# Two-layer Mamba and attention trunk: the first modulation pieces divided 5 to 3, the norm's spread ahead of the columns, and unit 0 between the time-step products

## The chip, the core and the metric

The kernel runs on one core of a Trainium2 chip. The metric is the device time of one execution in microseconds (us); the median of the runs is compared. The engines are TensorE (PE, with its weight loads as PEld), VectorE (DVE), ScalarE (ACT), GpSimd (POOL) and SyncE (SP), which issues every DMA.

## What is computed

Two layers of a decoder trunk on 512 tokens of width 1024, all in float32:

```
ada = silu(c) @ w_ada[l] + b_ada[l]             # six vectors of 1024: sh1, sc1, g1, sh2, sc2, g2
h = rms_norm(x, norm1_g[l]) * (1 + sc1) + sh1
z, xbc, dt_raw, q, k, v, gate_s, gate_a = split(h @ w_in[l])
y_ssm = mamba2(z, silu(conv(xbc)), softplus(dt_raw + dt_bias), ...) @ w_ssm_out[l]
y_att = diff_attention(q, k, v, ...) @ w_attn_out[l]
x = x + g1 * ((sigmoid(gate_s) * y_ssm + sigmoid(gate_a) * y_att) @ w_out[l])
x = x + g2 * (relu(norm_and_modulate(x, sc2, sh2) @ w_ff1[l]) ** 2 @ w_ff2[l])
```

The end is one more rms_norm. What matters here is the start of a layer: the modulation `sh1`, `sc1`, the norm of x, the raw time steps `dt_raw` (32 columns of the input projection), their softplus and running sums, and the first units of the projection, which feed the convolution.

## The kernel before

The model dimension lies on the partitions in 8 blocks (KB) of 128, the 512 tokens along the free dimension. Each weight matrix is cut into **units** of 256 output columns. A unit is loaded in two halves into `raw` (SP), copied by ScalarE to `w_hi` (L901), and POOL subtracts the two for `w_lo` (L1746), so that float32 products are made of three: hi by hi, hi by lo, lo by hi (L553 to L555). `unit_rows` issues the six products of one block k of a unit, three for each of its two banks; eight such **parts** make a unit. Unit n uses slot n % 2 of the weights and banks gemm 0, 1 or 2, 3; it may not start before unit n - 2 has left its banks (`bank_free`). For the units of the convolution it is VectorE's third tap (L1410, `taps`) that frees them.

Order is written out by hand on each engine, with semaphores between them. The middle of a layer goes by ticks from T_FIRST = -10; `fill_of(tick)` says how many parts TensorE issues in a tick, four each in the first ones, so ticks -10 and -9 hold unit 0, and -8 and -7 unit 1.

**Modulation pieces.** The vector `ada` is computed in pieces of 256 columns; the first eight (FIRST, layer 0) give `sh1` and `sc1` and are needed before the first norm. Each piece is 1 MB of weights. A TensorE piece is 16 small products with one column (`ada_piece`, L605; the trace counts each twice). A VectorE piece is eight multiply-adds into `ada_acc[:, n % 2]` (L1286, L1290), and TensorE then sums its partitions in two products (`ada_column`, L613). The accumulator has two halves, and the VectorE piece n begins with

```
dve.wait_ge(ada_out, n - 1 + OUT_CREDIT)      # OUT_CREDIT = 2; each ada_column adds 1
```

that is, when column n - 2 is done. When the last column is in, `ada_full` releases VectorE's `take_ada` (L1297) and ScalarE's first conversion of a weight unit, since the TensorE pieces lay in the place of `w_hi` and `w_lo`.

**Norm of layer 0.** ScalarE squares x, VectorE adds the squares (L1267, L1269), TensorE sums over partitions (`norm_sum`, L626), VectorE scales (`norm_mean`, L1276), POOL takes the power (L1734), TensorE spreads the result over partitions (`norm_spread`, L634). Then `norm` goes over the eight blocks: VectorE makes `pre` (L1316), ScalarE `h_hi` (L928), VectorE `h_lo` (L1321).

**Time steps.** As `h_lo` of block k arrives, TensorE makes its three products with `dtw` (L664 to L666). After the last, ScalarE adds the bias (L965) and takes an exponential, and VectorE's chain makes the softplus and running sums from it (L1366 to L1399). Only behind that chain does VectorE's program have the taps of unit 0 (L1410). TensorE meanwhile goes on with units 0 and 1.

## Time and profile before

| | |
|---|---|
| median of 3 runs | 2591.09 us (2589.17 to 2594.97) |
| profiled execution | 2592.25 us, span 2590.5 us |
| TensorE busy | 2391.4 us, 92% |
| VectorE busy | 1417.7 us, 55% |
| ScalarE busy | 1007.8 us, 39% |
| POOL busy | 1090.6 us, 42% |
| mean rate of the transfers | 97 GB/s |

The span is the profiled execution from its first to its last instruction. A row of the timeline has start, duration, engine, line and operation, the tiles written and read, and in brackets how long the engine had been idle and who ended it. Runs of equal instructions are merged into one row (xN). Busy time of one engine is no bound by itself; what counts is which wait ends last at each place.

### The profile page before, as it was taken

The numbers are of one execution on the slowest core, as the hardware profiler recorded it, in microseconds if no ns is written. First come the engines' busy times: TensorE is split into PE (matmuls) and PEld (weight loads), VectorE is DVE, ScalarE is ACT, GpSimd is POOL, SyncE is SP. The second block draws the span as 40 slices with busy tenths as digits, with TensorE's granted clock in tenths as the row PEclk, the third lists the DMA queues.
The fourth block names the chain that finished last, engine by engine and source line by source line (L and its number), as shares of the span: only waits on it lengthen the run. The fifth ranks groups of instructions, "written<-read, shape, count | busy, mean of one in ns | idle before, by whom it ended". The sixth has DMA issues, their size and how long they took to land.

```text
span 2590.5 us, 32150 instructions
## 1 busy us (share of the span) xinstructions
PE 2391.4 (92%) x11866; PEld 1960.3 (76%) x11866; DVE 1417.7 (55%) x2047; ACT 1007.8 (39%) x1864; POOL 1090.6 (42%) x825
## 2 busy tenths in 40 slices
PE   7899998997789989999988999999878899899998
PEld 6677897876666868888866778988666678688886
DVE  6766666445554447778767676622555534422323
ACT  3355553344444233322334555533444443322322
POOL 1355543432223445454434645454322244444442
PEclk9899999998989989999999999999988999899999
DMA  6211124511111434455422121232111123222221
GB/s 231 77 58 51 65 81 130 195 66 49 58 41 66 147 114 166 179 195 191 167 97 67 52 71 50 80 100 90 49 57 49 57 86 118 74 97 98 94 94 57
DMA packets 84812, 250.27 MB, mean 97 GB/s; under 512 B 7472, under 2 KB 34480, under 8 KB 79280
## 3 DMA queue, kind: packets, MB, share of 16 engines
q1 hardware_dynamic: 84656, 248.22, 28.3%
q8 instruction: 94, 1.54, 0.2%
q14 instruction: 62, 0.51, 0.1%
HBM read 244.00 MB, written 4.19 MB: 96 GB/s over the span
## 4 chain that ended last, share of the span: by engine, by line
PE 42%; issue 21%; POOL 9%; DVE 9%; POOLq 8%; ACT 5%; DVEq 3%; DMA 1%; ACTq 1%; SPq 0%
POOL w_lo L1746 9%; POOLq L1748 8%; PE gemm L553 8%; PE gemm L555 8%; PE gemm L554 8%; PE aux L714 3%; PE gemm L576 2%; PE gemm L577 2%; PE gemm L578 2%; PE aux L618 2%; ACT swap L1059 2%; ACT probs L1116 1%; PE aux L701 1%; DVE smalls L1604 1%; PE aux L725 1%
## 5 line engine op out<-in xcount | busy, mean ns | idle before, releaser
L1746 POOL TENSOR_TENSOR w_lo<-raw,w_hi 128x512 fp32r<-128x512 f32 x704 | 965.1, 1392 | 1357.7 <-ACT w_hi L901 1350.5
L901 ACT ACTIVATE w_hi<-raw 128x1024 fp32r<-128x1024 f32 x352 | 371.0, 1057 | 759.3 <-PE gemm L555 692.2
L553 PE MATMUL gemm<-h_hi,w_hi 128*128 128x512 f32 x1504 | 619.2, 412 | 25.1 <-DVE conv L1410 19.7
L555 PE MATMUL gemm<-h_hi,w_lo 128*128 128x512 f32 x1504 | 598.3, 398 | 0.0
L554 PE MATMUL gemm<-h_lo,w_hi 128*128 128x512 f32 x1504 | 598.1, 398 | 0.0
L553 PEld LDWEIGHTS gemm<-h_hi,w_hi 128*128 128x128 f32 x1504 | 290.8, 193 | 108.5 <-issue 51.0
L555 PEld LDWEIGHTS gemm<-h_hi,w_lo 128*128 128x128 f32 x1504 | 289.7, 193 | 64.4
L554 PEld LDWEIGHTS gemm<-h_lo,w_hi 128*128 128x128 f32 x1504 | 290.7, 193 | 58.4 <-issue 1.9
L553 PE MATMUL gemm<-op_hi,w_hi 128*128 128x512 f32 x608 | 238.5, 392 | 0.2
L555 PE MATMUL gemm<-op_hi,w_lo 128*128 128x512 f32 x608 | 236.8, 389 | 0.0
L554 PE MATMUL gemm<-op_lo,w_hi 128*128 128x512 f32 x608 | 236.6, 389 | 0.0
L576 PE MATMUL gemm<-w_hi,h_hi 128*128 128x256 f32 x768 | 230.1, 300 | 3.8 <-ACT zh L1033 2.2
L577 PE MATMUL gemm<-w_hi,h_lo 128*128 128x256 f32 x768 | 220.8, 287 | 0.0
L578 PE MATMUL gemm<-w_lo,h_hi 128*128 128x256 f32 x768 | 220.6, 287 | 0.0
L1290 DVE SCALAR_TENSOR_TENSOR late_acc<-ada_late,first,late_acc 128x256 f32<-128x256 f32 x210 | 157.0, 748 | 7.5
L576 PEld LDWEIGHTS gemm<-w_hi,h_hi 128*128 128x128 f32 x768 | 151.6, 197 | 12.1 <-issue 12.0
L1116 ACT ACTIVATE probs<-aux,smalls 128x128 f32<-128x128 f32 (+3 forms) x128 | 66.4, 524 | 239.4 <-DVEq L1594 238.6
L577 PEld LDWEIGHTS gemm<-w_hi,h_lo 128*128 128x128 f32 x768 | 151.4, 197 | 2.5 <-issue 2.4
L578 PEld LDWEIGHTS gemm<-w_lo,h_hi 128*128 128x128 f32 x768 | 150.7, 196 | 0.0
L1000 ACT ACTIVATE seg<-aux,tok 128x128 f32<-128x128 f32 x256 | 73.3, 369 | 195.2 <-PE aux L714 184.4
L1694 DVE TENSOR_TENSOR usq<-relu 128x512 f32<-128x512 f32 x64 | 66.2, 1034 | 143.8 <-ACTq L1215 140.9
L1714 DVE SCALAR_TENSOR_TENSOR x<-gemm,ada,x 128x512 f32<-128x512 f32 x64 | 45.9, 748 | 162.2 <-PE gemm L555 154.2
(195 smaller groups left out, 3522.6 us busy)
## 6 DMA issues: line engine op xcount, KB each, us to landing
raw<-stream SPq DMA_DIRECT2D x336, 512.0 KB
ada_late<-stream SPq DMA_DIRECT2D x30, 1024.0 KB, 4.8
ada_early<-stream SPq DMA_DIRECT2D x40, 256.0 KB, 3.9
raw<-stream SPq DMA_DIRECT2D x32, 256.0 KB
ada_pe<-stream SPq DMA_DIRECT2D x4, 1024.0 KB, 16.3
ada_first<-stream SPq DMA_DIRECT2D x4, 1024.0 KB, 18.2
x<-xT SPq DMA_DIRECT2D x2, 2048.0 KB, 10.9
xsave<-x SPq DMA_DIRECT2D x1, 2048.0 KB, 7.4
```

The costliest lines, as they stand in the source:

```text
L553: mm(o, w_hi[:, slot, k, cols], hi[:, k, :], start=k == 0, stop=False)
L554: mm(o, w_hi[:, slot, k, cols], lo[:, k, :], start=False, stop=False)
L555: last = mm(o, w_lo[:, slot, k, cols], hi[:, k, :], start=False, stop=k == KB - 1)
L576: mm(o, h_hi[:, k, toks], w_hi[:, slot, k, :], start=k == 0 and t % 2 == 0, stop=False, skip_group_check=True)
L577: mm(o, h_lo[:, k, toks], w_hi[:, slot, k, :], start=False, stop=False, skip_group_check=True)
L578: last = mm(o, h_hi[:, k, toks], w_lo[:, slot, k, :], start=False, stop=k == KB - 1, skip_group_check=True)
L714: last = mm(b[:, t * P + (r % 2) * HD:t * P + (r % 2 + 1) * HD], seg[:, r % 2, t, :], xdt[:, t, r % HG * HD:(r % HG + 1) * HD], start=True ...
L901: A(w_hi[:, slot, ks], raw[:, slot, ks], ACT.Copy).then_inc(hi_ready, 1)
L1116: A(probs[:, j % 2, part, 0:(j + 1) * P], ab[part][:, 0:(j + 1) * P], ACT.Exp, scale=AD ** -0.5, bias=mxn[:, col:col + 1], accum_out=den[: ...
L1290: STT(acc[:, n % 2], where[:, k], cact[:, k:k + 1], acc[:, n % 2], ALU.mult, ALU.add)\
L1746: gp.tensor_tensor(w_lo[:, slot, ks], raw[:, slot, ks], w_hi[:, slot, ks].bitcast(F32), ALU.subtract)
L1748: pool.drain().then_inc(lo_ready, 1)
```

## The change

VectorE takes five of the first eight pieces (0, 1, 2, 3, 7) and TensorE three (4, 5, 6); the transfers alternate from a VectorE piece on, and the eighth, a VectorE piece, lies where TensorE's fourth did. On TensorE, the first column comes before the norm's sum, and the spread before the other four columns. VectorE takes the mean after its third piece instead of before its second. In both layers, part k of unit 0 is issued behind the time-step products of block k, the last part after the flag that the time steps are complete; ticks -10 and -9 then issue nothing.

```diff
--- before.py
+++ after.py
@@ -87,10 +87,10 @@
 X_BEFORE = {4: 2, 5: 1, 7: 5, 8: 4, 10: 8, 11: 7}
 
 
-FIRST = [(0, m) for m in (4, 0, 5, 1, 6, 2, 7, 3)]
+FIRST, FIRST_PE = [(0, m) for m in (0, 1, 2, 3, 7)], [(0, m) for m in (4, 5, 6)]
 EARLY = [(0, m) for m in range(8, 18, 2)]
 LATE = [(0, m) for m in range(18, 24)] + [(1, m) for m in range(ADA)]
-N_FIRST, N_EARLY, N_LATE = len(FIRST) // 2, len(EARLY), len(LATE)
+N_FIRST, N_EARLY, N_LATE = len(FIRST), len(EARLY), len(LATE)
 N_LATE_AO = 2
 ADA_G2 = LATE.index((0, ADA - 1))
 EARLY_BUFS = 3
@@ -283,9 +283,10 @@
 
 
         ada_first = [place("ada_first0", [P, KB, UW], F32, r_a), place("ada_first1", [P, KB, UW], F32, r_a + 4 * T2),
-                     place("ada_first2", [P, KB, UW], F32, r_g), place("ada_first3", [P, KB, UW], F32, r_g + 4 * T2)]
+                     place("ada_first2", [P, KB, UW], F32, r_g), place("ada_first3", [P, KB, UW], F32, r_g + 4 * T2),
+                     place("ada_first4", [P, KB, UW], F32, r_lo + 4 * T2)]
         ada_pe = [place("ada_pe0", [P, KB, UW], F32, r_hi), place("ada_pe1", [P, KB, UW], F32, r_hi + 4 * T2),
-                  place("ada_pe2", [P, KB, UW], F32, r_lo), place("ada_pe3", [P, KB, UW], F32, r_lo + 4 * T2)]
+                  place("ada_pe2", [P, KB, UW], F32, r_lo)]
         ada_early = [place(f"ada_early{n}", [P, 2, 2 * UW], F32, r_a + n * 2 * T2) for n in range(EARLY_BUFS)]
         early_acc = place("early_acc", [P, 2, 2 * UW], F32, r_a + EARLY_BUFS * 2 * T2)
         ada_late = [place("ada_late0", [P, KB, UW], F32, r_a), place("ada_late1", [P, KB, UW], F32, r_a + 4 * T2)]
@@ -359,7 +360,7 @@
         aux_free = [sem(f"aux_free{b}") for b in range(4)]
 
         first_in = [sem(f"first_in{n}") for n in range(N_FIRST)]
-        pe_in = [sem(f"pe_in{n}") for n in range(N_FIRST)]
+        pe_in = [sem(f"pe_in{n}") for n in range(len(FIRST_PE))]
         early_in = [sem(f"early_in{n}") for n in range(EARLY_BUFS)]
         late_in = [sem("late_in0"), sem("late_in1")]
         ada_step, ada_out = sem("ada_step"), sem("ada_out")
@@ -461,8 +462,9 @@
 
             sp.dma_start(con[:], consts).then_inc(con_in, 16)
             for n in range(N_FIRST):
-                piece(ada_pe[n], *FIRST[2 * n], pe_in[n])
-                piece(ada_first[n], *FIRST[2 * n + 1], first_in[n])
+                piece(ada_first[n], *FIRST[n], first_in[n])
+                if n < len(FIRST_PE):
+                    piece(ada_pe[n], *FIRST_PE[n], pe_in[n])
                 if n == 0:
                     sp.dma_start(x[:], xT).then_inc(x_in, 16)
                     load_par(0)
@@ -641,30 +643,21 @@
                     norm_spread(st)
 
                 if l == 0:
-                    for n in range(N_FIRST):
+                    for n in range(2):
                         pe.wait_ge(pe_in[n], 16)
-                        ada_piece(ada_pe[n], ab[3], 2 * FIRST[2 * n][1])
-                        if n == 1:
-                            norm_sum(st)
-                        if n:
-                            ada_column(n - 1, ada_acc, ab[3], 2 * FIRST[2 * n - 1][1])
-                    ada_column(N_FIRST - 1, ada_acc, ab[3], 2 * FIRST[2 * N_FIRST - 1][1])
+                        ada_piece(ada_pe[n], ab[3], 2 * FIRST_PE[n][1])
+                    ada_column(0, ada_acc, ab[3], 2 * FIRST[0][1])
+                    norm_sum(st)
+                    pe.wait_ge(pe_in[2], 16)
+                    ada_piece(ada_pe[2], ab[3], 2 * FIRST_PE[2][1])
+                    norm_spread(st)
+                    for n in range(1, N_FIRST):
+                        ada_column(n, ada_acc, ab[3], 2 * FIRST[n][1])
                     pe.drain().then_inc(ada_full, 1)
-                    norm_spread(st)
                     pe.wait_ge(sel_ready, 1)
                 else:
 
                     pe.wait_ge(ada_read, 6)
-
-                st("bank2")
-                b = ab[2]
-                pe.wait_ge(S_["dtw"], st.at("dtw", 1) + 1)
-                for k in range(KB):
-                    pe.wait_ge(S_["h_lo"], st.at("h_lo", k) + 1)
-                    mm(b[:], dtw_hi[:, k, :], h_hi[:, k, :], start=k == 0, stop=False)
-                    mm(b[:], dtw_hi[:, k, :], h_lo[:, k, :], start=False, stop=False)
-                    last = mm(b[:], dtw_lo[:, k, :], h_hi[:, k, :], start=False, stop=k == KB - 1)
-                last.then_inc(aux_full[2], 1)
 
                 def dt_to_tokens():
                     b = aux(st, 3)
@@ -694,6 +687,19 @@
                     for p in range(first, first + count):
                         mid_part(p)
                     return first + count
+
+                st("bank2")
+                b = ab[2]
+                pe.wait_ge(S_["dtw"], st.at("dtw", 1) + 1)
+                for k in range(KB):
+                    pe.wait_ge(S_["h_lo"], st.at("h_lo", k) + 1)
+                    mm(b[:], dtw_hi[:, k, :], h_hi[:, k, :], start=k == 0, stop=False)
+                    mm(b[:], dtw_hi[:, k, :], h_lo[:, k, :], start=False, stop=False)
+                    last = mm(b[:], dtw_lo[:, k, :], h_hi[:, k, :], start=False, stop=k == KB - 1)
+                    if k < KB - 1:
+                        mid_part(k)
+                last.then_inc(aux_full[2], 1)
+                mid_part(KB - 1)
 
                 def spread(r):
 
@@ -775,9 +781,10 @@
                             if p == N_EARLY - 1:
                                 pe.drain().then_inc(ada_full, 1)
 
-                at = 0
+                at = KB
                 for tick in range(T_FIRST, T_ATT):
-                    at = fill(at, fill_of(tick))
+                    if tick >= T_FIRST + 2:
+                        at = fill(at, fill_of(tick))
                     if tick == -6:
                         dt_to_tokens()
                     if 0 <= tick + 2 < T_POST:
@@ -1270,8 +1277,9 @@
                     settle()
                     step("sq_used")
 
-            def norm_mean(step):
-                dve.drain().then_inc(S_["ss"], 1)
+            def norm_mean(step, summed=False):
+                if not summed:
+                    dve.drain().then_inc(S_["ss"], 1)
                 b = full(step, 0)
                 TS(ms[:], b[:, 0:TB], 1.0 / D, EPS, ALU.mult, ALU.add).then_inc(aux_free[0], 1)
                 dve.drain().then_inc(S_["ms"], 1)
@@ -1342,9 +1350,11 @@
                 if l == 0:
                     ada_piece(0, ada_first[0], (first_in[0], 16), ada_acc)
                     norm_add(st, range(KB))
-                    norm_mean(st)
+                    dve.drain().then_inc(S_["ss"], 1)
                     for n in range(1, N_FIRST):
                         ada_piece(n, ada_first[n], (first_in[n], 16), ada_acc)
+                        if n == 2:
+                            norm_mean(st, True)
                     dve.wait_ge(par_in, 16)
                     of_params(st)
                     dtw_low(st)
```

How this moves TensorE's instructions at the start of layer 0. Before (L605 a TensorE piece, L613 columns, L626 the norm's sum, L634 the spread):

```order
L605 MATMUL aux<-first,ada_pe_94 128x1 x16
L626 MATMUL aux<-first,ss 128x1 x4
L613 MATMUL aux<-first,ada_acc 128x1 x2
L605 MATMUL aux<-first,ada_pe_95 128x1 x16
L613 MATMUL aux<-first,ada_acc 128x1 x2
L605 MATMUL aux<-first,ada_pe_96 128x1 x16
L613 MATMUL aux<-first,ada_acc 128x1 x4
L634 MATMUL aux<-con,smalls 128x128 x4
```

And with the change, from the same point on (the lines are now L607, L615, L628, L636):

```order
L607 MATMUL aux<-first,ada_pe_95 128x1 x16
L615 MATMUL aux<-first,ada_acc 128x1 x2
L628 MATMUL aux<-first,ss 128x1 x4
L607 MATMUL aux<-first,ada_pe_96 128x1 x16
L636 MATMUL aux<-con,smalls 128x128 x4
L615 MATMUL aux<-first,ada_acc 128x1 x8
```

One column stands ahead of the norm's sum, and the other four (x8, two products each) have moved together behind the last piece and the spread.

VectorE at the same place with the change (L1294, L1298 a piece, L1276 the norm's additions, L1284 the mean):

```order
L1276 TENSOR_TENSOR ss<-ss,sq 128x512 [waits s_sq] x7
L1294 TENSOR_SCALAR ada_acc<-ada_first_90,first 128x256 [waits ada_out,first_in1]
L1298 SCALAR_TENSOR_TENSOR ada_acc<-ada_first_90,first,ada_acc 128x256 [waits ada_step] x7
L1294 TENSOR_SCALAR ada_acc<-ada_first_91,first 128x256 [waits ada_out,first_in2]
L1298 SCALAR_TENSOR_TENSOR ada_acc<-ada_first_91,first,ada_acc 128x256 [waits ada_step] x7
L1284 TENSOR_SCALAR smalls<-aux 128x4 [waits aux_full0]
L1294 TENSOR_SCALAR ada_acc<-ada_first_92,first 128x256 [waits ada_out,first_in3]
```

The mean, which stood ahead of the piece 90, is behind the piece 91; each piece still begins with a wait for `ada_out`.

TensorE at the end of the time-step products, before (aux2 is their bank, gemm0 and gemm1 those of unit 0):

```order
L664 MATMUL aux2<-h_hi_52,dtw_hi_82 128x512
L665 MATMUL aux2<-h_lo_53,dtw_hi_82 128x512
L666 MATMUL aux2<-h_hi_52,dtw_lo_83 128x512
L553 MATMUL gemm0<-h_hi_52,w_hi_50 128x512
L554 MATMUL gemm0<-h_lo_53,w_hi_50 128x512
L555 MATMUL gemm0<-h_hi_52,w_lo_51 128x512
```

With the change:

```order
L555 MATMUL gemm1<-h_hi_52,w_hi_50 128x512
L556 MATMUL gemm1<-h_lo_53,w_hi_50 128x512
L557 MATMUL gemm1<-h_hi_52,w_lo_51 128x512
L696 MATMUL aux2<-h_hi_52,dtw_hi_82 128x512
L697 MATMUL aux2<-h_lo_53,dtw_hi_82 128x512
L698 MATMUL aux2<-h_hi_52,dtw_lo_83 128x512
L555 MATMUL gemm0<-h_hi_52,w_hi_50 128x512
L556 MATMUL gemm0<-h_lo_53,w_hi_50 128x512
L557 MATMUL gemm0<-h_hi_52,w_lo_51 128x512
```

Seven parts of unit 0, 42 products, now stand ahead of the last three products of the time steps, and one part behind them.

## Rows read from the trace of the kernel before

**Rows 1.** Page of the kernel before, part 1: busy time (share of the span) and instructions.

```profile
PE 2391.4 (92%) x11866; PEld 1960.3 (76%) x11866; DVE 1417.7 (55%) x2047; ACT 1007.8 (39%) x1864; POOL 1090.6 (42%) x825
```

**Rows 2.** Timeline of TensorE, first product of unit 2, layers 0 and 1: start, us, engine, line.

```profile
92.78 0.77 PE L553 MATMUL gemm<-h_hi,w_hi 128*128 128x512 f32 x1 [10.22 <-DVE conv L1410]
...
1379.00 0.77 PE L553 MATMUL gemm<-h_hi,w_hi 128*128 128x512 f32 x1 [9.44 <-DVE conv L1410]
```

**Rows 3.** Timeline of VectorE, the chain of the time steps, layer 0.

```profile
62.95 1.14 DVE L1366 TENSOR_SCALAR dt_s<-dt_e 32x512 f32<-32x512 f32 x1
64.16 3.34 DVE L1368 RECIPROCAL dt_s<-dt_s 32x512 f32<-32x512 f32 x1
67.58 1.72 DVE L1370 TENSOR_TENSOR dt_s<-dt_e,dt_s 32x512 f32<-32x512 f32 x1
...
87.69 4.94 DVE L1410 SCALAR_TENSOR_TENSOR conv<-gemm,cw,conv 128x511 f32<-128x511 f32 x6
```

**Rows 4.** Timeline of VectorE, start of layer 0.

```profile
14.81 5.40 DVE L1269 TENSOR_TENSOR ss<-ss,sq 128x512 f32<-128x512 f32 x7
...
35.37 0.35 DVE L1286 TENSOR_SCALAR ada_acc<-ada_first,first 128x256 f32<-128x256 f32 x1 [0.33 <-PE aux L613]
...
39.28 0.21 DVE L1327 TENSOR_SCALAR cw<-par 128x120 f32<-128x120 f32 x1
...
40.05 1.22 DVE L1338 TENSOR_TENSOR dtw_lo<-dtw_raw,dtw_hi 128x1024 fp32r<-128x1024 f32 x1
...
46.13 1.41 DVE L1316 SCALAR_TENSOR_TENSOR pre<-x,amul,aux 128x512 f32<-128x512 f32 x2 [1.79 <-PE aux L634]
```

**Rows 5.** Issues of SyncE: its timeline, and the transfers of that window (KB, us to landing).

```profile
4.21 0.49 SPq L422 DMA_DIRECT2D ada_first<-stream  x1
...
ada_first<-stream SPq DMA_DIRECT2D x1, 1024.0 KB, 16.3
```

**Rows 6.** Timeline of TensorE, start of layer 0.

```profile
18.03 6.99 PE L605 MATMUL aux<-first,ada_pe 128*128 128x1 f32 x32 [4.71 <-DMA ada_pe<-stream]
24.88 1.85 PE L626 MATMUL aux<-first,ss 128*128 128x1 f32 x8
...
34.26 0.99 PE L613 MATMUL aux<-first,ada_acc 128*128 128x1 f32 x4
...
44.05 2.04 PE L634 MATMUL aux<-con,smalls 128*128 128x128 f32 x8 [0.26 <-issue]
49.64 0.77 PE L664 MATMUL aux<-h_hi,dtw_hi 128*128 128x512 f32 x1 [3.55 <-DVE h_lo L1321]
...
50.63 0.63 PE L666 MATMUL aux<-h_hi,dtw_lo 128*128 128x512 f32 x1
...
54.23 0.50 PE L664 MATMUL aux<-h_hi,dtw_hi 128*128 128x512 f32 x1
...
60.39 0.40 PE L666 MATMUL aux<-h_hi,dtw_lo 128*128 128x512 f32 x1
```

**Rows 7.** Timeline of POOL, the `w_lo` of unit 0 and unit 1, layer 0, and later.

```profile
45.01 2.50 POOL L1746 TENSOR_TENSOR w_lo<-raw,w_hi 128x512 fp32r<-128x512 f32 x2 [16.87 <-ACT w_hi L901]
...
62.52 2.72 POOL L1746 TENSOR_TENSOR w_lo<-raw,w_hi 128x512 fp32r<-128x512 f32 x2 [0.18 <-issue]
67.47 2.99 POOL L1746 TENSOR_TENSOR w_lo<-raw,w_hi 128x512 fp32r<-128x512 f32 x2 [2.23 <-ACT w_hi L901]
```

**Rows 8.** Busy time by windows, layer 0, then layer 1: window, us, PE (instructions), PEld, DVE, ACT, POOL, PEclk.

```profile
60.80:82.50 21.70, 21.70 (x96) 17.66 (x95) 20.54 (x19) 6.46 (x8) 13.45 (x10) 1.00 0.31 97
...
92.70:98.50 5.80, 5.72 (x14) 4.51 (x15) 4.44 (x7) 2.91 (x4) 2.53 (x2) 0.50 0.07 13
...
1336.60:1341.00 4.40, 4.34 (x9) 2.49 (x9) 4.20 (x6) 1.87 (x3) 1.04 (x1) 0.50 1.00 339
```

**Rows 9.** Timeline of VectorE, the same chain in layer 1.

```profile
1350.45 3.34 DVE L1368 RECIPROCAL dt_s<-dt_s 32x512 f32<-32x512 f32 x1
1353.87 0.68 DVE L1370 TENSOR_TENSOR dt_s<-dt_e,dt_s 32x512 f32<-32x512 f32 x1
```

## The prediction

> **What bounds the kernel now.** I read the page first: TensorE is busy for 92% of the span [rows 1], so a change in the start of a layer counts only if it moves the time at which TensorE goes on. The timeline of TensorE gives that time. After the products of the time steps (L664 to L666) and units 0 and 1 it stands still for 10.2 us in layer 0 and 9.4 us in layer 1, and both times VectorE's `conv` (L1410) ends the wait [rows 2]: unit 2 needs the banks of unit 0, which the taps of unit 0 free. VectorE's own timeline says why the taps are late. The chain of the time steps (L1366 to L1399) stands ahead of them, begins 2.2 us after the last product of the time steps, and has no gap [rows 3]. So **the path goes: normalised blocks, last product of the time steps, VectorE's chain, taps, unit 2**. Units 0 and 1 lie beside it and have about 10 us to spare. Ahead of it, the start of layer 0 is a race: the norm began on VectorE at 46.13 us [rows 4].
>
> **Part 1, the pieces and the spread (layer 0 only).** The eight pieces are loaded in the same eight places of the queue, and slots keep their landing times; slot 4, now TensorE's second piece, was issued at 4.21 and landed 16.3 us later, at 20.5 [rows 5]. A piece costs TensorE 6.85 us (18.03 to 24.88), a column about 0.9, the norm's sum 1.85, the spread 2.04 [rows 6]; it costs VectorE 3.91 us (35.37 to 39.28) [rows 4]. What decides is a rule in the code: VectorE's accumulator has two halves, and piece n may begin only when column n-2 has been summed. Row 35.37 shows that wait being served by TensorE's L613, 0.33 us [rows 4], 0.1 us after the column of 34.26 had ended [rows 6]. In the new order column 1 stands behind the third TensorE piece and behind the spread. Worked through:
> TensorE: second piece 20.5 to 27.4, column 0 to 28.3, norm's sum to 30.1, third piece 30.0 to 36.8, spread to 39.1, column 1 to 40.0.
> VectorE: the norm's additions end at 20.2 as before [rows 4]; piece 1 to 24.2; piece 2 waits for column 0, 28.4 to 32.3; the mean; piece 3 waits for column 1, **40.1 to 44.0**; piece 4 to 47.9. The parameters and `dtw_lo` take 2.0 us (39.28 to 41.27) [rows 4], to 49.9; the last column is done at 49.0, inside that. Reading the sums and the scale takes some 0.6 us, and the first `pre` starts at about 50.6, against 46.13: **+4.5 us**. The spread, which ended the wait of 1.79 us there, is now early, but what it waited with is later. ScalarE's first conversion of unit 0 and POOL's `w_lo` (45.01 before) [rows 7] hang on the same flag and move from about 44 and 45 to 49 and 50, so the 3.5 us from the first `pre` to the first product (46.13 to 49.64) [rows 4, 6] stay. Bounds: +3.5 if the columns come half a microsecond early at each turn, +6 if the 2.0 us conversion holds the first `h_hi` back.
>
> **Part 2, unit 0 between the products (both layers).** 42 products of unit 0 (six after each of the first seven blocks) now stand ahead of the last time-step product. Before, the 24 products were paced by VectorE's `h_lo`, one block in 1.5 us, and ended 11.15 us after the first (49.64 to 60.39 and 0.40) [rows 6]. Now 66 products run without a gap. The clock first: in layer 1 the first 4.40 us of these products have a granted clock of 0.50, the lower of the two levels, 1.2 GHz [rows 8]; in layer 0 products start 0.43 us apart (0.99 from 49.64 to 50.63, the first step a little longer) until 54.2 [rows 6], and later 96 of them fill 21.70 us at 2.4 GHz, 0.226 each [rows 8]. At the lower level about 10.4 products start in 4.6 us; the other 55.6 take 12.6 us; with the last one's tail 17.3 us. The last time-step product is **6.15 us later** in each layer. Before, the cold stretch cost nothing, because VectorE was the slower; now it costs. Bounds: +3.9 (no cold stretch, 66 by 0.226), +7.5 (cold for 5.8 us, as at the restart of unit 2 [rows 8], and 0.1 us at each change between the two kinds). The six products of each block that are taken out from behind (10.9 us of unit 0, less six) save nothing: they were beside VectorE's chain. TensorE's wait before unit 2 grows from 10 to some 18 us.
> In front of the first interleaved product stands a wait for unit 0's `w_lo`; its first half should be ready near 53, the first product is due near 54.2. I cost it at nothing; 1 us of margin covers it in layer 0, and in layer 1 it is long ready.
>
> **Part 3, what the chain meets.** VectorE's chain lasted 26.9 us in layer 0, from the last product's end (60.79) [rows 6] to the taps (87.69) [rows 3]. Its instructions come in two lengths: L1370 took 1.72 us at 67.58, just after POOL had begun a half of `w_lo` at 67.47, and 0.68 in layer 1, where POOL was idle [rows 3, 7, 9]. The reciprocal took 3.34 in both, though in layer 0 POOL ran into it until 65.24 [rows 3, 7, 9]. So an instruction that meets POOL costs some 1.0 more, the reciprocal nothing, and a half (two POOL instructions) catches two of them, some 1.95. Four halves lie beside the chain in layer 0 (the first two of them in [rows 7], two like them at 72.9 and 78.4); the first catches only L1366, 1.14 instead of 0.42. That makes 0.7 + 3 x 1.95 = 6.5 us, and 5.8 in layer 1, which has three. After the change unit 1's `w_lo` is over before the chain begins, and unit 2's first half, which may be converted at once, falls on the reciprocal; two halves remain, 3.9 us. So **-2.6 us in layer 0 and -1.9 in layer 1**. Bounds: nothing saved, to all of 6.5 and 5.8 saved.
> The Trainium skill (SBUF — State Buffer, "Who interferes with whom") has it that a VectorE instruction with two SBUF inputs and a GpSimd instruction that reads SBUF exclude each other for the whole instruction. By that rule two halves would cost the full 2.5 us each, 5.1 instead of 3.9, and the sum would come out 2.4 us higher; the rows speak for the smaller figure: L1370 grew by 1.04 us where a POOL instruction lasts half of 2.5 [rows 3, 7, 9].
>
> **The sum.** Layer 0: 4.5 + 6.15 - 2.6 = 8.1. Layer 1: 6.15 - 1.9 = 4.2. Behind unit 2 everything hangs on TensorE and moves as one block, so nothing is won or lost there: **+12.3 us**. Against the profiled execution (2592.25, span 2590.5) 2604.5; it lies 1.2 above the median of the runs, and against that median I forecast **2603.4 us**.
>
> **The rivals.**
> (a) *The cost is fuller*: the clock rises later after the longer idle stretches and POOL keeps colliding. Layer 0: 4.5 + 6.7 - 0.5, layer 1: 6.7, sum +17.4, 2608.5. For it: the cold stretch of 5.8 us at another restart [rows 8], and the new halves of `w_lo` follow each other closely. Against it: 4.6 us at the place in question. 0.13.
> (b) *The column does not hold piece 3 up*: then VectorE's pieces 3 and 4 follow from 32.3 to 40.2, TensorE's last column ends at 42.6, and the norm begins at about 43.2, 2.9 us earlier instead of 4.5 later: +4.9, 2596.0. Against it stand the wait at 35.37 [rows 4] and the order of the columns. 0.04.
> (c) *Faster*: TensorE is the bound, as 92% suggests, and filling its gaps of 0.5 us between blocks is pure gain. Unit 0 would be finished 18.7 us after the first product (17.3 and one more block of 1.36) instead of 22.0, 3.3 us sooner in each layer; with the early spread of (b), 2.9 more, -9.5 and 2581.6. The point that decides is the wait before unit 2: it must be near zero, and it is 10.2 and 9.4 us, ended by VectorE [rows 2]. 0.02.
> (d) *Swallowed*: some later stretch is set by transfers, not by TensorE, and the delay disappears there; 2591, or up to 2594 if a quarter of it stays. The page's 92% and loads that themselves wait for `lo_ready` speak against it. 0.03.
> The forecast's own case has 0.78.
>
> **How the numbers follow.** A measurement of this kernel tells a difference from none above about 0.2%, 5.2 us. The forecast's case spans +6.5 to +18: its lower end takes the clock and POOL terms at their kind ends together, the upper the unkind ones of (a). The range 2597.3 to 2609.0 leaves out (b) to (d), 0.09, and about a tenth more at both ends. Faster by over 0.2%: (c), 0.02. Within 0.2%: (b) and (d), 0.07. Slower: 0.91.
>
> **What would show it.** Right: VectorE idle ahead of piece 3 from about 32.5 to 40, behind TensorE's column; first `pre` near 50.6; last time-step product 17.3 us after the first, in both layers; TensorE's wait before unit 2 at 18 us, still ended by `conv`; a chain of about 24.3 us. Wrong: a wait before unit 2 that shrinks, a column served before the spread, or a span that grows by less than the shift of unit 2's first product in layer 0 and layer 1 together.

## The result and the profile after

| | before | changed |
|---|---|---|
| median | 2591.51 us (2587.03 to 2594.97, 6 runs) | 2602.69 us (2600.81 to 2605.48, 6 runs) |
| span of the profiled execution | 2590.5 us | 2601.3 us |
| ratio of the two | | 1.0045 (95% interval 1.0032 to 1.0058) |

The change makes the kernel 11.2 us slower. The forecast was 12.3 us slower, 2603.4 us, with a range from 2597.3 to 2609.0; the measured 2602.69 lies in it. (The median of the kernel before is 2591.51 here and not 2591.09, since three more runs of it were added.)

TensorE's work is what it was, from the page of the changed kernel, part 1:

```profile
PE 2388.9 (92%) x11838; PEld 1963.4 (75%) x11838; DVE 1410.9 (54%) x2055; ACT 1007.3 (39%) x1864; POOL 1088.8 (42%) x825
```

It answers to [rows 1]: 28 records fewer, which are a TensorE piece less and a column more, and a busy time 2.5 us shorter, though the kernel is longer. The loss is idle time. TensorE's timeline at the start of layer 0, after:

```profile
20.52 6.99 PE L607 MATMUL aux<-first,ada_pe 128*128 128x1 f32 x32 [4.70 <-DMA ada_pe<-stream]
27.37 0.99 PE L615 MATMUL aux<-first,ada_acc 128*128 128x1 f32 x4
28.22 1.84 PE L628 MATMUL aux<-first,ss 128*128 128x1 f32 x8
29.93 6.97 PE L607 MATMUL aux<-first,ada_pe 128*128 128x1 f32 x32
36.76 2.05 PE L636 MATMUL aux<-con,smalls 128*128 128x128 f32 x8
38.60 1.71 PE L615 MATMUL aux<-first,ada_acc 128*128 128x1 f32 x8
43.62 1.01 PE L615 MATMUL aux<-first,ada_acc 128*128 128x1 f32 x4 [3.31 <-DVE ada_acc L1298]
...
52.95 0.76 PE L696 MATMUL aux<-h_hi,dtw_hi 128*128 128x512 f32 x1 [4.41 <-DVE h_lo L1329]
...
54.36 0.63 PE L555 MATMUL gemm<-h_hi,w_hi 128*128 128x512 f32 x1
...
56.92 0.63 PE L696 MATMUL aux<-h_hi,dtw_hi 128*128 128x512 f32 x1
...
59.50 0.39 PE L696 MATMUL aux<-h_hi,dtw_hi 128*128 128x512 f32 x1
...
70.17 0.39 PE L698 MATMUL aux<-h_hi,dtw_lo 128*128 128x512 f32 x1
...
99.65 0.77 PE L555 MATMUL gemm<-h_hi,w_hi 128*128 128x512 f32 x1 [16.86 <-DVE conv L1420]
```

Against [rows 6]: column 0 at 27.37 comes before the norm's sum, and columns 1 and 2 (one row, x8) at 38.60 come behind the spread. Columns 3 and 4 wait for VectorE's pieces (3.31 us at 43.62, and again ahead of the last). The first time-step product starts at 52.95 instead of 49.64, and the last ends at 70.56 (70.17 and 0.39) instead of 60.79. The wait before unit 2 has grown from 10.22 us [rows 2] to 16.86, still ended by `conv`. VectorE's side of the same stretch, its timeline:

```profile
28.47 0.35 DVE L1294 TENSOR_SCALAR ada_acc<-ada_first,first 128x256 f32<-128x256 f32 x1 [3.99 <-PE aux L615]
...
39.56 0.35 DVE L1294 TENSOR_SCALAR ada_acc<-ada_first,first 128x256 f32<-128x256 f32 x1 [7.02 <-PE aux L615]
...
43.48 0.35 DVE L1294 TENSOR_SCALAR ada_acc<-ada_first,first 128x256 f32<-128x256 f32 x1
...
49.83 1.41 DVE L1324 SCALAR_TENSOR_TENSOR pre<-x,amul,aux 128x512 f32<-128x512 f32 x2
...
72.71 0.42 DVE L1376 TENSOR_SCALAR dt_s<-dt_e 32x512 f32<-32x512 f32 x1 [6.31 <-ACT dt_e L976]
73.20 3.34 DVE L1378 RECIPROCAL dt_s<-dt_s 32x512 f32<-32x512 f32 x1
76.62 1.64 DVE L1380 TENSOR_TENSOR dt_s<-dt_e,dt_s 32x512 f32<-32x512 f32 x1
78.33 1.63 DVE L1382 TENSOR_TENSOR dt_s<-dt_s 32x512 f32<-32x512 f32 x1
...
94.57 4.93 DVE L1420 SCALAR_TENSOR_TENSOR conv<-gemm,cw,conv 128x511 f32<-128x511 f32 x6
```

Piece 2 waits 3.99 us for column 0, piece 3 waits 7.02 us for column 1 (`PE aux L615`, the new line of the columns); before, that wait was 0.33 us [rows 4]. The first `pre` is at 49.83 instead of 46.13. Then VectorE stands idle for 6.31 us until the last time-step product has come through ScalarE, where before it had none of that [rows 3]. The chain itself, from the end of the last time-step product to the taps, goes from 70.56 to 94.57, 24.0 us instead of 26.9. In layer 1 the interleaving alone is at work, TensorE's timeline:

```profile
1340.84 0.77 PE L696 MATMUL aux<-h_hi,dtw_hi 128*128 128x512 f32 x1 [2.47 <-DVE h_lo L1329]
...
1357.10 0.39 PE L696 MATMUL aux<-h_hi,dtw_hi 128*128 128x512 f32 x1
...
1357.56 0.39 PE L698 MATMUL aux<-h_hi,dtw_lo 128*128 128x512 f32 x1
...
1387.03 0.77 PE L555 MATMUL gemm<-h_hi,w_hi 128*128 128x512 f32 x1 [16.84 <-DVE conv L1420]
```

Last time-step product 17.1 us after the first (before 11.1), wait before unit 2 16.84 us instead of 9.44 [rows 2].

### The profile page after: what moved, and what is told of

Same layout as the page of the kernel before. It is cut to its first block, busy times and chain, and to the rows that moved or that the text cites. A ratio compares the mean times of both kernels' runs of the same rounds, so it can differ in the third digit from the quotient of the medians.

```text
span 2601.3 us, 32103 instructions
## 1 busy us (share of the span) xinstructions
PE 2388.9 (92%) x11838; PEld 1963.4 (75%) x11838; DVE 1410.9 (54%) x2055; ACT 1007.3 (39%) x1864; POOL 1088.8 (42%) x825
## 4 chain that ended last, share of the span: by engine, by line
PE 44%; issue 21%; POOL 9%; DVE 8%; POOLq 8%; ACT 5%; DVEq 3%; DMA 1%; ACTq 1%; SPq 0%; PEldq 0%; PEld 0%
POOL w_lo L1756 9%; PE gemm L555 8%; POOLq L1758 8%; PE gemm L556 8%; PE gemm L557 8%; PE gemm L578 3%; PE gemm L579 3%; PE gemm L580 3%; PE aux L720 3%; PE aux L620 2%; ACT swap L1066 2%; ACT probs L1123 1%; PE aux L811 1%; PE aux L707 1%; PE aux L731 1%
## 5 line engine op out<-in xcount | busy, mean ns | idle before, releaser
L578 PEld LDWEIGHTS gemm<-w_hi,h_hi 128*128 128x128 f32 x768 | 153.0, 199 | 12.0 <-issue 11.9
L1298 DVE SCALAR_TENSOR_TENSOR late_acc<-ada_late,first,late_acc 128x256 f32<-128x256 f32 x210 | 157.1, 748 | 7.5
```

The costliest lines, as they stand in the source:

```text
L578: mm(o, h_hi[:, k, toks], w_hi[:, slot, k, :], start=k == 0 and t % 2 == 0, stop=False, skip_group_check=True)
L1298: STT(acc[:, n % 2], where[:, k], cact[:, k:k + 1], acc[:, n % 2], ALU.mult, ALU.add)\
```

## The experiments

Every kernel was timed beside the kernel before, whose median stands in brackets. The kernels e1 to e4, e5 to e8 and e9 to e11 were timed together, e12 by itself. Beside the median stands what one trace of each kernel shows at the two places where TensorE goes on, as a difference to the kernel before: the start of unit 2 in layer 0 (92.78 us before), and in layer 1 the distance from the first `pre` to the start of unit 2 (44.78 us before). The text calls the sum of the two what the places show.

| kernel | median (kernel before) | ratio, 95% interval | unit 2 of layer 0 | layer 1 | both |
|---|---|---|---|---|---|
| changed | 2602.69 (2591.51) | 1.0045, 1.0032 to 1.0058 | +6.9 | +3.9 | +10.7 |
| e1_front_only | 2594.23 (2589.68) | 1.0021, 1.0011 to 1.0030 | +3.5 | 0.0 | +3.5 |
| e2_interleave_only | 2595.86 (2589.68) | 1.0024, 1.0014 to 1.0034 | +2.6 | +4.0 | +6.6 |
| e3_columns_early | 2589.59 (2589.68) | 1.0006, 0.9997 to 1.0014 | -4.0 | +0.1 | -4.0 |
| e4_every_other | 2584.11 (2589.68) | 0.9980, 0.9971 to 0.9988 | -1.0 | -1.3 | -2.3 |
| e5_pool_behind_chain | 2577.41 (2589.00) | 0.9956, 0.9943 to 0.9969 | -6.0 | -5.9 | -11.9 |
| e6_taps_in_chain | 2578.33 (2589.00) | 0.9956, 0.9943 to 0.9970 | | | |
| e7_taps_interleave | 2595.57 (2589.00) | 1.0020, 1.0011 to 1.0029 | | | |
| e8_after_columns_early | 2595.00 (2589.00) | 1.0024, 1.0015 to 1.0033 | -1.6 | +4.1 | +2.5 |
| e9_columns_and_pool | 2576.02 (2590.17) | 0.9938, 0.9926 to 0.9951 | -10.0 | -5.9 | -15.9 |
| e10_interleave_pool | 2588.60 (2590.17) | 0.9992, 0.9984 to 1.0000 | -0.8 | +0.3 | -0.5 |
| e11_taps_pool_half | 2574.77 (2590.17) | 0.9935, 0.9923 to 0.9947 | | | |
| e12_all_three | 2573.38 (2590.31) | 0.9936, 0.9922 to 0.9950 | | | |

(For the kernels with the taps inside the chain unit 2 starts in another order, so no such number is given.)

**Each half of the change alone.** e1_front_only takes the interleaving back (the diff in part; the time-step products also move back ahead of `dt_to_tokens`):

```diff
-                    if k < KB - 1:
-                        mid_part(k)
                 last.then_inc(aux_full[2], 1)
-                mid_part(KB - 1)
...
-                at = KB
+                at = 0
                 for tick in range(T_FIRST, T_ATT):
-                    if tick >= T_FIRST + 2:
-                        at = fill(at, fill_of(tick))
+                    at = fill(at, fill_of(tick))
```

> The front of the change alone (pieces 5 to 3, spread ahead of the columns), unit 0 back behind the time-step products. If the late column is what costs: VectorE's piece 3 starts near 39.6, the first product of the time steps near 53.0, 3.3 us later than before, and the whole kernel 3 to 4 us slower (ratio 1.0013). If interleaving is harmless and the front alone carries the loss: 11 us slower.

e2_interleave_only puts the same lines into the kernel before.

> Unit 0 between the time-step products, in both layers, with the front as before. If VectorE's chain is the path: last time-step product 6.0 to 6.5 us later, a chain of 24.0 us instead of 26.9 and 26.1, unit 2 at +3.6 us in layer 0 and +3.9 more in layer 1, sum +7.5 (ratio 1.0029), and TensorE's wait before unit 2 of 16.9 us. If TensorE is the bound and filled gaps are a gain: 3.3 us less in each layer, 6.6 us faster.

Measured +4.6 and +6.2 us in the medians, where 3 to 4 and 7.5 were expected. The places agree with the first theory of each. TensorE's timeline of e1, first time-step product and first product of unit 2:

```profile
52.97 0.76 PE L667 MATMUL aux<-h_hi,dtw_hi 128*128 128x512 f32 x1 [4.41 <-DVE h_lo L1325]
...
96.27 0.77 PE L555 MATMUL gemm<-h_hi,w_hi 128*128 128x512 f32 x1 [10.22 <-DVE conv L1416]
```

And the same two rows of e2:

```profile
49.54 0.76 PE L693 MATMUL aux<-h_hi,dtw_hi 128*128 128x512 f32 x1 [3.55 <-DVE h_lo L1325]
...
95.34 0.77 PE L553 MATMUL gemm<-h_hi,w_hi 128*128 128x512 f32 x1 [16.86 <-DVE conv L1414]
```

In e1 the first time-step product is 3.3 us later than before, and the wait before unit 2 is the old 10.22. In e2 the front is the old one and the wait has grown to 16.86. The halves add up to 10.7 of the 11.2 us (4.55 and 6.18). The rivals (all of the loss in the front; a gain from filled gaps) are refuted.

**The column's place.** e3_columns_early keeps 5 to 3 and the early mean, and moves TensorE's columns:

```diff
                     pe.wait_ge(pe_in[0], 16)
                     ada_piece(ada_pe[0], ab[3], 2 * FIRST_PE[0][1])
+                    ada_column(0, ada_acc, ab[3], 2 * FIRST[0][1])
+                    norm_sum(st)
                     pe.wait_ge(pe_in[1], 16)
                     ada_piece(ada_pe[1], ab[3], 2 * FIRST_PE[1][1])
-                    ada_column(0, ada_acc, ab[3], 2 * FIRST[0][1])
-                    norm_sum(st)
+                    ada_column(1, ada_acc, ab[3], 2 * FIRST[1][1])
+                    ada_column(2, ada_acc, ab[3], 2 * FIRST[2][1])
+                    norm_spread(st)
                     pe.wait_ge(pe_in[2], 16)
                     ada_piece(ada_pe[2], ab[3], 2 * FIRST_PE[2][1])
-                    norm_spread(st)
-                    for n in range(1, N_FIRST):
+                    for n in range(3, N_FIRST):
```

> Pieces 5 to 3 without interleaving, but column 0 and the norm's sum ahead of TensorE's second piece, columns 1 and 2 behind it, the spread ahead of the third piece, columns 3 and 4 last. If the late column was the cause: VectorE's pieces 3 and 4 start near 30 and 34, the last piece of TensorE ends near 40, ada_full near 41.5, the first pre near 42.0 against 46.13, and the kernel is about 4 us faster than before (ratio 0.9984). If the 5 to 3 division or the early spread themselves cost: 3 us slower, as with the front of the change.

VectorE's timeline of e3:

```profile
24.43 0.35 DVE L1293 TENSOR_SCALAR ada_acc<-ada_first,first 128x256 f32<-128x256 f32 x1
...
30.06 0.35 DVE L1293 TENSOR_SCALAR ada_acc<-ada_first,first 128x256 f32<-128x256 f32 x1 [1.57 <-PE aux L615]
...
33.98 0.35 DVE L1293 TENSOR_SCALAR ada_acc<-ada_first,first 128x256 f32<-128x256 f32 x1
...
41.68 1.41 DVE L1323 SCALAR_TENSOR_TENSOR pre<-x,amul,aux 128x512 f32<-128x512 f32 x2
```

Piece 3 waits 1.57 us instead of 7.02, and the first `pre` is at 41.68, 8.2 us before that of the changed kernel. The division of the pieces and the spread ahead of the third TensorE piece are the same in both kernels, so it is the place of the columns that cost the front its time. The expectation for the whole kernel (4 us faster) was missed, though: -4.0 us in front of unit 2 of layer 0, and nothing in the median. The shift is lost again later; more on that below. e8_after_columns_early makes the same edit, with the same diff, in the changed kernel.

> The changed kernel with the columns placed early as in e3. If the two costs of the change add up: unit 2 starts 1.5 us earlier than before in layer 0 (-4.0 from the front, +2.6 from interleaving) and loses 3.9 us more in layer 1, sum +2.4 us against before, 8.5 us less than the change. If the front's loss was caused by interleaving or by the 5 to 3 division: still about +10 us.

Measured +6.0 against before, where +2.4 was expected: a miss. The places add as expected (-1.6 and +4.1), but the median is 3.5 us above their sum. So of the 11.2 us the better place of the columns takes back 5.2 in the median, and 8.2 by the places.

**The dose.** e4_every_other puts three parts between instead of seven, starting from the kernel before (the diff in part; the block also moves behind `mid_part`, and ticks -10 and -9 issue nothing, as in the change):

```diff
                     last = mm(b[:], dtw_lo[:, k, :], h_hi[:, k, :], start=False, stop=k == KB - 1)
+                    if k % 2 and k < KB - 1:
+                        mid_part(k // 2)
                 last.then_inc(aux_full[2], 1)
+                for k in range(KB // 2 - 1, KB):
+                    mid_part(k)
```

> The dose made smaller: parts 0, 1, 2 of unit 0 behind the time-step products of blocks 1, 3, 5, the other five behind the last; front as before. 18 products of unit 0 stand ahead of the last time-step product instead of 42. If the path is the last time-step product and the chain: it comes about 1 us later (42 products in 12.2 us against 11.15), and the chain meets POOL once less (-1.9 us), so 0 to 2 us faster over both layers. If interleaving costs by itself, in proportion: +3 us; if it gains by filling gaps: -3 us.

The time-step products take 12.9 us in layer 0 and 12.0 in layer 1 (11.15 and 11.14 before), and the chain 24.2 and 24.0 us (26.9 and 26.1). That gives the -2.3 us of the table. TensorE's wait before unit 2 grows all the same:

```profile
91.76 0.77 PE L553 MATMUL gemm<-h_hi,w_hi 128*128 128x512 f32 x1 [11.64 <-DVE conv L1415]
```

The cost in proportion (+3 us) is refuted. The gain in proportion (-3 us) is not told from the theory of the path by this run's total, but it is refuted by e2, where more than twice as many products between cost 6 us: the sign turns with the dose. The median is -5.6, where 0 to -2 was expected; 3.3 us of it have no cause that the places show.

**POOL and the chain.** e5_pool_behind_chain is the kernel before with

```diff
                     for part in HALVES_AT[tick]:
+                        if part == 4:
+                            pool.wait_ge(S_["dt_v"], l * TOTAL["dt_v"] + 1)
                         low(l, part // 2, part % 2)
```

> The kernel before, with POOL's w_lo of unit 2 (and so all after it) waiting until VectorE's chain of the time steps is done. If meeting POOL is what lengthens VectorE's instructions by about 1 us each: the chain shrinks from 26.9 and 26.1 to about 21.0 and 20.4 us, unit 2 starts some 5.8 us earlier in each layer (its w_lo is ready 3 us after the chain, the taps end 5 us after it), sum -11 to -12 us (ratio 0.9955). If VectorE's two lengths have another cause: chain as before, 0 us; if the delayed w_lo holds TensorE up later, slower.

VectorE's timeline of e5, the chain in layer 0:

```profile
67.52 0.68 DVE L1370 TENSOR_TENSOR dt_s<-dt_e,dt_s 32x512 f32<-32x512 f32 x1
68.27 0.68 DVE L1372 TENSOR_TENSOR dt_s<-dt_s 32x512 f32<-32x512 f32 x1
69.02 0.41 DVE L1374 TENSOR_SCALAR dt_p<-dt_s 32x512 f32<-32x512 f32 x1
...
81.70 4.93 DVE L1410 SCALAR_TENSOR_TENSOR conv<-gemm,cw,conv 128x511 f32<-128x511 f32 x6
```

POOL's timeline of e5, unit 2's first half:

```profile
81.68 2.50 POOL L1746 TENSOR_TENSOR w_lo<-raw,w_hi 128x512 fp32r<-128x512 f32 x2 [16.50 <-DVEq L1401]
```

And TensorE's timeline of e5, start of unit 2:

```profile
86.78 0.77 PE L553 MATMUL gemm<-h_hi,w_hi 128*128 128x512 f32 x1 [4.29 <-DVE conv L1410]
```

With POOL idle, L1370 takes 0.68 us where it took 1.72 [rows 3]; the chain shrinks to 21.0 us (81.70 less 60.72) and to 20.3 in layer 1, and the kernel is 11.6 us faster, as expected. This tests what the third term of the prediction rests on, and with e6 it is the largest single gain of the study. TensorE still waits 4.29 us, for the chain without its meetings.

e10_interleave_pool adds the interleaving (the lines of e2) to e5:

> Interleaving in both layers with POOL behind the chain, so that no chain meets POOL. This measures the delay of the last time-step product alone: against e5, 5.6 to 6.5 us later in layer 0 and 6.1 in layer 1, about 12 us slower than e5, and equal to before (0 to +1 us). If what interleaving costs is only a matter of POOL and the chain: equal to e5.

The time-step products take 16.8 and 17.3 us (11.1 in e5), and the chain 20.2 in both layers, against 21.0 and 20.3 in e5, whose first still met unit 1's `w_lo`. TensorE's timeline of e10, start of unit 2:

```profile
91.96 0.76 PE L553 MATMUL gemm<-h_hi,w_hi 128*128 128x512 f32 x1 [13.07 <-DVE conv L1414]
```

Against e5 unit 2 is 5.2 us later in layer 0 and layer 1 loses 6.1, 11.3 together, where about 12 were expected; the ratios to before, 0.9956 and 0.9992, differ by 9.3 us. So most of the delay of the last time-step product, by the places all of it, is paid. In the change a part of it was hidden by POOL and VectorE meeting less.

**Where the taps stand.** e6_taps_in_chain (the diff in part; the function `taps` also moves up unchanged, ahead of the chain):

```diff
                 for odd in (15, 13, 11, 9, 7, 5, 3):
                     settle()
                     STT(dt_p[:], dt_p[:], 1.0 / odd, dt_s2[:], ALU.add, ALU.mult)
+                    if odd == 9:
+                        taps(0, 0)
+                        taps(0, 1)
...
-                    for n in since(tick, 0, U_Z, 1):
+                    for n in since(tick, 1, U_Z, 1):
                         taps(n, 0)
```

> The kernel before, with the taps of unit 0 inside VectorE's chain (behind the fourth multiply-add of L1377) instead of behind it. If only the place of the taps makes TensorE wait before unit 2: that wait goes, and a wait of about 4.6 us for the chain's end stands before the time steps' transposes in the middle of unit 2; TensorE is 7 to 8 us further in each layer, sum -14 to -16 us (ratio 0.994). If TensorE's wait has another cause: no change.

e7_taps_interleave adds the lines of e2 to it.

> The kernel of e6_taps_in_chain with unit 0 between the time-step products in both layers. If the last time-step product and the chain are the path even without the wait before unit 2: 3 to 4 us slower than e6 in each layer, 7 us in sum. If interleaving is a gain as soon as TensorE's wait before unit 2 is gone (rival c of the prediction): 3.3 us faster than e6 in each layer.

e6 is 10.7 us faster than before. The wait before unit 2 is gone, and TensorE's timeline has the expected wait before the transposes:

```profile
94.42 0.87 PE L673 MATMUL aux<-con,dt_rows 96*128 96x96 f32 x4 [6.54 <-DVEq L1418]
```

It is 6.54 us, and 5.61 in layer 1, not 4.6: the chain is longer by the taps, and four halves of `w_lo` still meet its small instructions in layer 0 and lengthen two each. The two waits make some 2.9 of the 3.3 us by which the gain falls short of the expected 14 to 16. At the transposes TensorE is 6.6 us further in layer 0 (94.42 against 101.06). e7, with the interleaving, is 17.2 us slower than e6, where 7 were expected. TensorE's timeline of e7, start of unit 2 and the transposes:

```profile
87.45 0.76 PE L553 MATMUL gemm<-h_hi,w_hi 128*128 128x512 f32 x1 [7.55 <-DVE conv L1375]
...
100.51 0.87 PE L663 MATMUL aux<-con,dt_rows 96*128 96x96 f32 x4 [4.65 <-DVEq L1422]
```

The later chain brings the wait before unit 2 back (7.55 us, the taps starting at 82.39 instead of 76.26) on top of the wait before the transposes (4.65). By the start of the transposes e7 is 6.1 us behind e6 in layer 0 and, counted from the first `pre`, 6.4 in layer 1; the remaining 4.7 us of the medians have no cause that these places show. The direction decides against rival (c): even with the taps moved, interleaving costs.

**Towards a faster kernel.** e9_columns_and_pool joins e3 and e5. e11_taps_pool_half joins e4, e6 and a softer form of e5 (POOL waits before part 5, so that unit 2's first half falls on the reciprocal). e12_all_three adds the front of e3 to e11. The only new line is e11's, here against e5:

```diff
-                        if part == 4:
+                        if part == 5:
                             pool.wait_ge(S_["dt_v"], l * TOTAL["dt_v"] + 1)
```

> Columns early (e3) and POOL behind the chain (e5) together, no interleaving. Both act on the path in front of unit 2 and should add: unit 2 of layer 0 about 10 us earlier than before (4.0 and 5.9), layer 1 gains 6 to 7 more, so 16 to 18 us faster than before (ratio 0.9935). If the time that e3 did not show at the end is lost again in the stages with idle TensorE: 11 to 13 us faster, no better than e5 alone.

> A version meant to be fast: three parts of unit 0 between the products (e4), unit 0's taps inside the chain (e6), POOL free to make unit 2's first half beside the reciprocal and waiting for the chain's end with the rest. A chain with taps of about 25.3 us, TensorE waiting some 2 us before the transposes and 2 us before unit 2's second half: 1.5 to 2 us better than e5 in each layer, 14 to 16 us faster than before. If the late w_lo of unit 2's second half weighs more: no better than e5.

> e11 with the front of e3 (columns early). In front of unit 2 of layer 0 another 4 us should go: 18 to 21 us faster than before (ratio 0.992). If e3's gain is lost again later, as it was there: 15 to 16 us, equal to e11.

Measured: 14.2, 15.4 and 16.9 us faster in the medians; the three intervals lie on each other (0.9938, 0.9935, 0.9936), and e9's overlaps that of e5 alone. By the places e9 had 15.9 us, the lower end of the expected 16 to 18; its median lies between that and the 11 to 13 of its rival. So among these three no one is shown to be the fastest, and what the columns add to e5 is not clear of the noise. e11's two waits come out as planned, in TensorE's timeline:

```profile
88.54 0.52 PE L663 MATMUL aux<-con,dt_rows 96*128 96x96 f32 x4 [2.54 <-DVEq L1423]
91.51 0.79 PE L553 MATMUL gemm<-h_hi,w_hi 128*128 128x512 f32 x1 [2.44 <-POOLq L1756]
```

e12, with 16.9 us, missed the lower bound of its expectation (18) by a microsecond: e3's front again showed little in the end.

## Why the prediction was right

**Part 1, the column.** Right in mechanism. VectorE's piece 3 started at 39.56 (forecast 40.1), the first `pre` at 49.83 (50.6). The term was 4.5 us and measured 3.7, and at the first product 3.3. Of the 0.8 us that the forecast was too high, 0.5 was there when piece 3 began, since the spread and the column behind it took less than assumed (column 1 was done near 39.5, not 40.0); the rest came in small steps behind it. ScalarE's conversion of unit 0 ran until 50.62, just until the first `pre` was ready, and held nothing back: `h_hi` began 0.78 us after `pre` in both kernels. What shortened the distance from `pre` to product from 3.5 to 3.1 us is the first `h_lo`, 1.44 us instead of 1.83. e1 and e3 show that it is the column.

**Part 2, the products.** Forecast 17.3 us from the first to the last time-step product and 6.15 us of delay; measured 17.6 and 17.1, delays of 6.5 and 6.0. The slow stretch is visible in TensorE's rows: the first two blocks start 3.97 us apart (52.95 and 56.92), the next 2.58, the last ones 2.04. In layer 0 it is read from the spacing of the products alone (0.43 us, as in layer 1 at a granted clock of 0.50), for the profile's clock says 1.00 there. Its length in layer 0 was not the same in every execution: 2.7 us in e2 (last product 16.7 us after the first), 4.8 in the changed kernel (17.6), 5.7 in e7 (18.1). So the forecast's 4.6 was a middle case, and that it came so near is partly luck. TensorE's wait before unit 2 was 16.9 us, not some 18; the prediction's own terms give 17.1 (10.2 + 6.15 - 2.6 + 3.3). e10 against e5 confirms the term alone. The products were continuous, and the `w_lo` of unit 0, which I had costed at nothing, was ready in time: unit 0's first part followed the first three products without a wait.

**Part 3, POOL.** Forecast -2.6 and -1.9; measured 26.90 - 24.01 = 2.9 and 26.12 - 24.00 = 2.1 us. What still meets POOL costs 24.01 - 20.22 = 3.8 us against e10, whose chain meets nothing; the forecast had 3.9. In the changed kernel POOL's first half of unit 2 ran from 73.71 to 76.26 beside the reciprocal, which still took 3.34 us, and the next two instructions, L1380 and L1382, took 1.64 and 1.63 where e5 has 0.68 for each. The trace puts the cost at about 0.95 us per instruction met. POOL's timeline of the changed kernel, taken one instruction at a time, shows why it is this much:

```profile
76.43 1.29 POOL L1756 TENSOR_TENSOR w_lo<-raw,w_hi 128x512 fp32r<-128x512 f32 x1 [0.18 <-issue]
77.68 1.74 POOL L1756 TENSOR_TENSOR w_lo<-raw,w_hi 128x512 fp32r<-128x512 f32 x1
```

L1380 (76.62 to 78.26) ended 0.54 us after the POOL instruction it had met (77.72), and L1382 (78.33 to 79.96) 0.54 us after the next (79.42), which had itself grown from 1.3 to 1.74 us. That is the picture of two engines that take turns, each waiting for the rest of the other's instruction. So the rule of the Trainium skill (SBUF — State Buffer, "Who interferes with whom"), exclusion for a whole instruction, agrees with this trace. What was wrong is the prediction's working from it, a full 2.5 us for each half, which would have made the chain 1.2 us longer than it was: VectorE waits only for what is left of POOL's instruction when it comes, and POOL waits for VectorE in turn.

**The sum.** 3.5 + 2.6 for the halves in layer 0 gives 6.1, the changed kernel had 6.9 there, and 3.9 in layer 1, together 10.7; forecast 8.1 + 4.2 = 12.3, measured 11.2. In the changed kernel's own rows layer 0 is 3.3 + 6.5 - 2.9 = 6.9. The terms that were too high are that of part 1, by 1.2, and that of layer 1, by 0.3.

**What was wrong** is the sentence "Behind unit 2 everything hangs on TensorE and moves as one block, so nothing is won or lost there". In the profiled executions unit 2 of layer 0 was 6.9 us late and the first time-step product of layer 1 only 4.2 (1340.84 against 1336.66), and after unit 2 of layer 1 (8.0 late) the end was 10.8 late. The 2.7 us lost and found cancel in the sum here, and that is luck. In e3 they did not: a shift of 4.0 us vanished in a median of 11 runs. In its profiled execution unit 2 of layer 1 was even 6.6 us early (1372.41), and the end only 2.9 (2587.6 against 2590.5), so the loss lies behind it. Busy time by windows (window, us, PE, PEld, DVE, ACT, POOL, then PEclk, DMA share, GB/s), first from unit 2 of layer 1 to the end, then a stretch within it, of the kernel before:

```profile
1379.00:2590.50 1211.50, 1134.95 (x5653) 930.28 (x5653) 547.70 (x800) 482.47 (x902) 521.18 (x396) 0.96 0.23 76
...
2050.00:2250.00 200.00, 183.13 (x823) 147.30 (x822) 82.51 (x132) 70.77 (x123) 81.76 (x63) 0.96 0.26 89
```

And of e3, the second stretch begun 6.6 us earlier like its program:

```profile
1372.41:2587.60 1215.19, 1140.04 (x5653) 934.44 (x5653) 546.90 (x800) 482.40 (x902) 520.75 (x396) 0.96 0.24 76
...
2043.40:2243.40 200.00, 182.79 (x808) 146.76 (x807) 82.32 (x131) 68.67 (x119) 80.96 (x62) 0.94 0.26 85
```

The same 5653 products keep TensorE busy for 5.1 us longer in e3, and the stretch lasts 3.7 us longer, while none of TensorE's waits in it has grown by more than 0.4 us. The granted clock, the third number from the end, is 0.96 and 0.94 in the shorter stretch; of 200 us that is about 4 us of the full clock, and 15 products fewer fit in. Over the whole execution, by the figure that each run gives, it was 0.9631 in the mean of 29 runs of before and 0.9605 in 11 of e3; 0.0026 of 2590 us is 6.7 us of the full clock, enough for what is missing. In e4, which did better than its places, it was 0.9648. So the clock granted in the later stages accompanies these residues, also in e8 (0.9605 against 0.9635 before). e9 does not follow it: 0.9638 against 0.9622, and 1.7 us worse than its places. Why a kernel whose later program is the same, only shifted by some microseconds, should systematically be granted less is not settled by these runs.

**The range** was worked out wrongly at its lower end. The prediction says that +6.5 us takes the terms of the clock and of POOL at their kind ends together. Its own bounds for these two give 4.5 + 3.9 - 6.5 and 3.9 - 5.8, together 0; +6.5 is about what the kind ends of the column and the clock give alone (3.5 + 3.9 - 2.6 and 3.9 - 1.9, together 6.8). The POOL bound was never near: 2.9 and 2.1 us were saved, not 6.5 and 5.8.

**The rivals.** (a), the fuller cost, did not come: the slow stretch in layer 0 was 4.8 us, against 4.6 before, and POOL did meet less. (b) is refuted by the wait of 7.02 us. (c) is refuted by the wait before unit 2, by e2 and by e7. (d) is refuted by the measured 11.2 us, though e3 shows that a single shift can vanish by the end, there with more busy time of TensorE and not in a wait for transfers.

## What to carry to other kernels

Ask of a gap that is to be filled who waits for the instruction behind it. TensorE's gaps between the time-step products were real, but the last of these products headed another engine's serial chain, and six products put into each gap of half a microsecond delayed it by 6 us, while what they brought forward had 10 us to spare. Three parts in these gaps instead of seven delayed it by 1.7 and 0.8 us and left the kernel 2.3 us faster by the places, 5.6 in the median. With a double-buffered accumulator, count where the release of the buffer stands in the other engine's order: moving it behind two longer jobs cost more than the better division of the work could give. And look at what the path's engine meets: one wait that kept POOL away from VectorE's chain was worth 11.6 us.

## What the runs showed of the hardware that was not expected

VectorE's small instructions with two inputs (32 x 512) cost 0.68 us alone and 1.6 to 1.7 beside POOL's subtraction of two SBUF tiles; a one-input multiply grows too, from 0.41 (L1374 before) to 1.36 us (L1384 in the changed kernel); the reciprocal does not, 3.34 us in every trace. Each instruction met ends some 0.3 to 0.5 us after the POOL instruction it met, and POOL's own instruction grows from 1.3 to as much as 1.74 us. The taps, which read the banks of unit 0, took 4.93 us in e5 beside POOL, as they did without it. Removing all of these meetings but one took the chain from 26.9 and 26.1 to 21.0 and 20.3 us.

Medians of this kernel follow shifts of its first stages only to about 3 to 5 us (e3, e4, e8), in both directions and beyond what the intervals allow, with the mean granted clock moving along; a local gain under 5 us here should be read from the place in the trace and from the clock, and not from the median alone.
